# A streaming encoder layer: expert choices every 16 ticks, own buffers for the queries, and a mixer in three banks

## The reference, cut to what matters

```python
z = rmsnorm(h);  p = z @ W_in                       # W_in: 1024 x 3080, fp32
h = h + concat(rglru_group(p), mlstm_group(p)) @ W_out   # the mixer
h = h + peer(rmsnorm(h))
y = rmsnorm(h)

def peer_block(xb):                                 # xb: 128 tokens x 1024
    qh = (xb @ wq).reshape(128, 8, 2, 128)          # 8 heads, two halves
    s1, s2 = qh[:, :, 0] @ keys1.T, qh[:, :, 1] @ keys2.T    # 128 keys each
    v1, i1 = top_k(s1, 16);  v2, i2 = top_k(s2, 16)
    sc, ci = top_k((v1[..., :, None] + v2[..., None, :]).reshape(128, 8, 256), 16)
    e = take(i1, ci // 16) * 128 + take(i2, ci % 16)         # 16 experts a head
    act = gelu(einsum('td,thkd->thk', xb, u_tab[e])) * softmax(sc)
    return einsum('thk,thkd->td', act, v_tab[e])
```

## Time and profile before

| | |
|---|---|
| Median of three runs | 3309.66 us (3309.31 to 3315.91) |
| The profiled execution, its own time | 3304.53 us |
| Its span in the profile | 3302.3 us |
| TensorE, VectorE, ScalarE, GpSimd busy | 79%, 69%, 20%, 61% |
| Mean granted TensorE clock | 0.852 |
| Read from memory, mean rate | 1205.73 MB, 367 GB/s |

### The profile page before, as it was taken

One profiled execution on the slowest core, in us unless ns is written; L12 is line 12 of the kernel. 1 busy time (PEld: TensorE's weight loads), 2 busy tenths in 40 slices (PEclk: granted clock), 3 DMA queues, 4 the chain that ended last, 5 costly groups with the idle time before them and its releaser, 6 DMA issues.

```text
span 3302.3 us, 42154 instructions
## 1 busy us (share of the span) xinstructions
PE 2607.0 (79%) x11764; PEld 1183.6 (36%) x11764; DVE 2282.9 (69%) x6088; ACT 648.6 (20%) x2367; POOL 2004.0 (61%) x2131
## 2 busy tenths in 40 slices
PE   7687888778887788778887788778887788777666
PEld 2563453234422453234422453234422453233111
DVE  2454987678756887679756887578766887679453
ACT  2221222111211222111211122112211222111111
POOL 0132567665776567665766567665776567665775
PEclk9798999878997889878987899878997889888557
DMA  7354999999999999999999999999999999999998
GB/s 263 135 197 166 387 363 394 416 390 344 396 405 403 377 368 395 409 391 349 399 402 398 376 368 398 407 392 343 404 413 400 371 368 399 403 398 359 398 399 362
DMA packets 340171, 1213.81 MB, mean 368 GB/s; under 512 B 41072, under 2 KB 41200, under 8 KB 339904
## 3 DMA queue, kind: packets, MB, share of 16 engines
q0 software_dynamic: 304128, 1107.43, 85.8%
q1 hardware_dynamic: 35776, 103.32, 8.3%
HBM read 1205.73 MB, written 4.87 MB: 367 GB/s over the span
## 4 chain that ended last, share of the span: by engine, by line
PE 25%; DMA 25%; DVE 24%; issue 15%; POOL 6%; ACT 3%; POOLq 0%; DVEq 0%; ACTq 0%; SPq 0%
DMA ring<-peer_v,idxv 16%; PE bank L458 15%; PE acc L458 10%; DMA ring<-peer_u,idx 9%; DVE ring L1434 8%; POOL ring L434 6%; DVE kw L1211 2%; DVE eh L1222 1%; DVE kw L1221 1%; DVE topi L1213 1%; DVE kw L1219 1%; ACT xn L857 1%; DVE idxv L1269 1%; DVE tops L1212 1%; DVE topi L1214 1%
## 5 line engine op out<-in xcount | busy, mean ns | idle before, releaser
L458 PE MATMUL acc<-ring,wv 128*32 128x512 f32 x4224 | 1312.9, 709 | 540.4 <-DMA ring<-peer_v,idxv 417.7
L1434 DVE SCALAR_TENSOR_TENSOR ring<-ring,xcur 128x1024 f32<-128x1024 f32 x1056 | 1283.6, 1218 | 656.4 <-DMA ring<-peer_u,idx 630.6
L434 POOL DMA_INDIRECT ring<-peer_u,idx x1056 | 1006.6, 953 | 817.7 <-issue 416.3
L434 POOL DMA_INDIRECT ring<-peer_v,idxv x1024 | 964.0, 941 | 433.5 <-issue 277.1
L458 PEld LDWEIGHTS acc<-ring,wv 128*32 128x32 f32 x4224 | 171.3, 115 | 1203.2 <-issue 662.7
L458 PEld LDWEIGHTS bank<-xT,win 128*128 128x128 f32 (+1 forms) x2304 | 276.2, 190 | 108.5 <-issue 92.9
L458 PE MATMUL bank<-xT,win 128*128 128x128 f32 (+1 forms) x2304 | 307.1, 290 | 6.8 <-DVE kw L1232 4.3
L857 ACT ACTIVATE wv<-rep,coefv 128x32 f32<-128x32 f32 x1024 | 264.3, 312 | 109.4 <-PE acc L458 79.4
L458 PEld LDWEIGHTS bank<-xT,qk 128*128 128x128 f32 x1024 | 160.1, 246 | 64.5 <-issue 64.5
L458 PE MATMUL bank<-win,xT 128*128 128x512 f32 (+3 forms) x368 | 177.3, 614 | 1.9 <-ACT xT L857 1.9
L458 PE MATMUL bank<-xT,qk 128*128 128x128 f32 x1024 | 173.1, 338 | 0.0
(11 more groups left out here) (232 smaller groups left out, 2213.8 us busy)
## 6 DMA issues: line engine op xcount, KB each, us to landing
qk<-wq SPq DMA_DIRECT2D x64, 512.0 KB
t<-wq SPq DMA_DIRECT2D x64, 512.0 KB, 6.9
ring<-peer_u,idx POOLq DMA_INDIRECT x1056, 6.5
ring<-peer_v,idxv POOLq DMA_INDIRECT x1024, 6.6
win<-w_in SPq DMA_DIRECT2D x6, 2048.0 KB, 15.3
ring<-wq SPq DMA_DIRECT2D x16, 512.0 KB, 5.2
wout<-w_out SPq DMA_DIRECT2D x1, 4096.0 KB, 22.4
xn<-x_prompt SPq DMA_DIRECT2D x8, 512.0 KB, 6.9
```

The source lines that it names most:

```text
L434: pool.indirect_dma_start(out=ring[:, slot, :], out_offset=None, in_=(peer_u, peer_v)[which], in_offset=bass.IndirectOffsetOnAxis(ap=rows_ ...
L458: return nc.tensor.matmul(out, lhsT, rhs, start=start, stop=stop)
L1434: stt(row, row, 1.0, xcur[:, :], ALU.mult, ALU.mult, accum_out=dots[:, column(b, e):column(b, e) + 1]).then_inc(s_dot, 1)
```

## The change

- A head's choice comes every 16 ticks: head h's first query product at tick 16h - 22, the second 3 ticks later, the scores at 16h - 13, the five steps at 16h - 12 to 16h - 8, the spread at 16h - 7. Heads 0 and 1 begin in the block before.
- Queries get buffers of their own: `wqb` (one, not two), `x2T`, `q2`, `pick`, and the PSUM bank bQ, which also takes both spreads. The mixer has bA, bC and bD.
- The mixer's ticks move: norm at 24 (30), convolution 38 (44), recurrence 49 (55), values 62 (66), chunk 70 (74), output 87 (91), second norm 101 (105). The waits between mixer and spreads go; some inside the mixer come, as the value projection's on the recurrence (`s_m2`).
- The lookup of a choice is one one-hot product over 512 columns, where there were two over 256.
- The norms' weights are columns. The second norm's are applied by ScalarE as it moves the transposed x; TensorE transposes that back into `xcur` (`show_x`) and spreads the final norm's row into bA and bC each block (`final_row`). ScalarE scales by the second norm's rstd, not VectorE.
- x is loaded into `h`, after `take_up`, not into `xn` after the store of y.

```diff
 HEAD_TICKS = TOPK
 BLOCK_TICKS = PEER_HEADS * HEAD_TICKS
-QUERY_TICKS = 5
-T_QUERY = 1
-T_NORM, T_XT, T_XT_OUT = 30, 35, 36
+Q_FIRST, Q_SECOND, Q_SCORES, Q_CHOOSE, Q_GATE, Q_SPREAD = 0, 3, 9, 10, 13, 15
+Q_LEAD = 22
+EARLY_HEADS = (0, 1)
+T_NORM, T_XT, T_XT_OUT = 24, 29, 30
...
-T_XL, T_GATES, T_GL, T_Q, T_K, T_V, T_O = 37, 43, 45, 52, 59, 66, 73
-T_CONV = 44
-T_ROWS = 46
-T_GELU = 51
-T_LRU = 55
-T_CHUNK = 74
-T_OUT = 91
-T_NORM2 = 105
-T_QUERY0 = 110
+T_XL, T_GATES, T_GL, T_Q, T_K, T_V, T_O = 31, 37, 39, 46, 53, 62, 69
+T_CONV = 38
+T_ROWS = 40
+T_GELU = 45
+T_LRU = 49
+T_CHUNK = 70
+T_OUT = 87
+T_NORM2 = 101
...
-        ffn_bc = sb("ffn_bc", [P, D_MODEL])
-        final_bc = sb("final_bc", [P, D_MODEL])
+        ffn = sb("ffn", [P, CM])
+        fin = sb("fin", [P, CM])
+        wqb = sb("wqb", [P, CM, P])
+        x2T = sb("x2T", [P, CM, P])
+        q2 = sb("q2", [P, 2, P])
+        pick = sb("pick", [P, 2 * TOPK * TOPK])
...
-        wq_buf = [qk, t34]
-        q2 = G
...
-        bank = [ctx.enter_context(nc.psum_tensor(f"bank{b}", [P, 512], fp32)) for b in range(4)]
-        bA, bB, bC, bD = bank
+        bA, bC, bD, bQ = [ctx.enter_context(nc.psum_tensor(f"bank{b}", [P, 512], fp32)) for b in "ACDQ"]
+        num_banks, c_banks, out_banks, x2_banks = (bA, bD), (bC, bA), (bA, bC), (bD, bA)
...
+        def query_step(head, tick):
+
+            return tick + Q_LEAD - HEAD_TICKS * head
...
             def load_wq(b, tiles):
                 for ft in tiles:
-                    if ft < 2:
-                        sp.wait_ge(s_ym_ps, streams_before(b) + 1)
-                    else:
-                        sp.wait_ge(s_qp_ps, b * 16 + ft - 1)
+                    if ft or not is_count(b, 0):
+                        sp.wait_ge(s_qp_ps, b * 16 + ft)
                     held()
-                    sp.dma_start(wq_buf[ft % 2][:, :, :], wq[ft]).then_inc(s_wq[ft % 2], 16)
+                    sp.dma_start(wqb[:, :, :], wq[ft]).then_inc(s_wq, 16)
...
             def load_x(b, block):
 
-                sp.wait_ge(s_xcur, streams_before(b))
+                sp.wait_ge(s_acc0, b + 1)
                 held()
-                sp.wait_ge(s_y_out, 16 * b)
-                held()
-                sp.dma_start(xn[:, :], block).then_inc(s_x, 16)
+                sp.dma_start(h[:, :], block).then_inc(s_x, 16)
...
                     if part == 0:
                         pe.wait_ge(s_win[4], 16)
-                        pe.wait_ge(s_ri_exp, v + 1)
+                        pe.wait_ge(s_m2, v + 1)
...
+                for half, at in enumerate((Q_FIRST, Q_SECOND)):
+                    if step == at:
...
+                        for c in range(CM):
+                            last = mm(bQ[:, P * half:P * half + P], wqb[:, c, :], x2T[:, c, :], start=c == 0, stop=c == CM - 1)
+                        last.then_inc(s_qp_ps, 1)
+                if step == Q_SCORES:
...
+                if step == Q_SPREAD:
...
+                    spread_rows(ef[:, :], s_idx_ps)
...
+            def show_x(b):
+
+                pe.wait_ge(s_x2, streams_before(b) + 1)
+                if b is not None:
+                    pe.wait_ge(s_dot, experts_before(b))
+                for c in range(CM):
+                    last = nc.tensor.transpose(xcur[:, P * c:P * c + P], x2T[:, c, :], ident[:, :])
+                last.then_inc(s_xcur, 1)
+
+            def final_row(b):
+
+                n = n_experts(b)
+                if b is None:
+                    pe.wait_ge(s_rows_bc, 32)
+                for c in range(CM):
+                    last = mm(by4((bA, bC)[c // 4])[0:n, c % 4, :], spread(fin[:, c:c + 1], 1, n), ident[:, :])
+                last.then_inc(s_fin, 1)
...
+                if tick % TOPK == 1 and tick > TOPK:
+                    spread_coef(b, tick // TOPK - 1)
                 for head in range(1, PEER_HEADS):
-                    query(b, head, tick - T_QUERY - QUERY_TICKS * (head - 1))
...
+                    query(b, head, query_step(head, tick))
                 if more:
+                    for head in EARLY_HEADS:
+                        query(b + 1, head, query_step(head, tick - BLOCK_TICKS))
                     mixer(b + 3, b + 2, P, True, tick, b)
...
-                    rstd(n, 3, D_MODEL).then_inc(s_rstd2, 1)
+                    link(rstd(n, 3, D_MODEL))
+                    a(xn[0:n, :], h[0:n, :], ACT.Copy, scale=stat[0:n, 5:6]).then_inc(s_xn2, 1)
...
-            def take_over(b):
...
-                    last = a(xcur[:, :], xn[:, :], ACT.Copy)
-                last.then_inc(s_xcur, 1)
...
-                    pick(0, temps)
+                    oh = one_hots(temp)
+                    link(tt(oh, ci[:, 1:3, :].unsqueeze(3).to_broadcast(square),
+                            iota[:, :].unsqueeze(1).unsqueeze(1).to_broadcast(square), ALU.is_equal))
+                    link(tt(oh, oh, topi[:, :, :].unsqueeze(2).to_broadcast(square), ALU.mult))
                 if step == 4:
-                    pick(1, temps)
+                    link(dve.tensor_reduce(eh[:, :, :], one_hots(temp), AX.X, ALU.add))
...
-                stt(y, y, stat[0:n, 8:9], final_bc[0:n, :], ALU.mult, ALU.mult).then_inc(s_y, 1)
+                dve.wait_ge(s_fin, streams_before(b) + 1)
+                for half, bank in enumerate((bA, bC)):
+                    y = xn[0:n, 512 * half:512 * half + 512]
+                    last = stt(y, y, stat[0:n, 8:9], bank[0:n, :], ALU.mult, ALU.mult)
+                last.then_inc(s_y, 1)
```

356 lines of the change are left out of this document (152 added, 204 removed).

## The result

The changed kernel takes 3453.56 us (median of 5 runs, 3433.92 to 3471.85), the kernel before 3309.31 on the same chip: a ratio of 1.0439, 95% interval 1.0392 to 1.0486. It is slower by 4.4%; forecast was 3287 us and the range ended at 3358. The execution that was profiled is the longest of the five, 3471.85 us, so differences between the two profiles are some 20 us larger than those of the medians.

The account below looks back on a forecast made before the run. Memory and GpSimd's gather issue, both about 420 GB/s, were taken as the bound. Seven passes at -2.6 us, last block -13 and start +8 gave -23, so 3287 us against a 3309.7 median; range 3225 to 3358.

Parts of the forecast that it names:

- How much lateness is free: Ring of 8 row buffers: VectorE or TensorE may be 3 us late (2.2 to 4.5) at no cost, then all lost.
- Part 1: Choices every 16 ticks: late at most 2.8 us, heads 1 and 2 cost 0.3 each; -10.4 us a pass.
- Part 2: Choices meeting the mixer: head 3 at the convolution +4.9, head 4 at the recurrence +2.1, heads 5 to 7 +2.1 us.
- Removed 11.0: Dense choices, ticks 5 to 14 and 21 to 41: their whole loss of 11.0 us a pass would go.
- their count at half: Heads 5 to 7: 4.3 us lost, entered as +2.1 because their stretch already loses 5.5.
- Part 3: Queries on TensorE in the mixer, ticks 29 to 58: 81.3 us of work against 79.7 of traffic, +1.6 us.
- rival B: Thinner ring, only 2.2 us free: 3339 us; second half, TensorE over 95% busy in ticks 29 to 58: to 3365; chance 0.22.
- Part 4: Turn of the loop, ticks 15 to 20: -2.4 us without arrears, -1.0 if the final row keeps TensorE's clock up.
- Part 5: Small items: showing x by TensorE transposes +0.5 us; single query-weight buffer no price, 0 to 0.5 us a head.
- a sign that held: Start of the kernel: growing by over 15 us was listed as a sign of the forecast being wrong.
- C: TensorE's clock: thinned queries at half clock bind TensorE outside the mixer, some 9 us a pass, 3359 us; chance 0.05.
- A: Lumps are absorbed by the ring, 4.5 us free: -10 a pass, -16 in the last block, 3231 us; chance 0.17.

Follow-up runs that it names:

- packed: Changed kernel with each choice's five steps in 3 ticks instead of 5; 3591.72 us, ratio 1.0856.
- spaced_copy: spaced with VectorE's copy of the spread choice one tick behind TensorE's spreading product, second query product a tick later too; 3324.96 us, 1.0051.
- align: Changed kernel with each head's first query tile load held back until the scores of the head before are there; 3451.53 us, 1.0401.
- conv44: Changed kernel with the convolution at ticks 44 and 45 instead of 38 and 39; 3428.45 us, 1.0386.
- copy_conv44: spaced_copy with the convolution at ticks 44 and 45 instead of 38 and 39; 3308.79 us, 1.0003.
- o_later: two_at_start with the projection of o two ticks later (71 to 76 instead of 69 to 74); 3303.36 us, 0.9969.
- two_at_start: x_early with the very first block's second query tile loaded early into qk; 3301.89 us, 0.9959.
- turn: Changed kernel with the final norm weights' spread moved ahead to tick 10 and SP storing y before loading the next x; 3464.59 us, 1.0466.
- second5: Changed kernel with a head's second query product 5 ticks after its first instead of 3; 3456.72 us, 1.0438.
- x_early: copy_conv44 with the sample's h copied to the idle query-weight buffer, so the first block's x loads earlier; 3309.63 us, 1.0011.
- spaced: Changed kernel with each choice's five steps at about every second tick, copy and gate later to match; 3364.96 us, 1.0141.

## Why the prediction was wrong

**The step that failed: "How much lateness is free".** It put 8 slots x 1.245 = 9.96 us against 6.5 for a row to land and 1.3 to be used, and took 3 us as free, at every lump anew. The runs put 0.9 us lost for each microsecond late between 0.5 and 6.1 us at head 7, and an allowance of at most about 1 us. The 6.5 us are no fixed delay but grow with the queue: the first eight gathers of the changed kernel's sample, with nothing queued ahead of them, land after 4.8 us, all of its u gathers after 6.9, packed's after 6.6 and those of spaced_copy, which keeps memory busiest of the three, after 7.2 (medians). That the queue is what keeps memory busy while an engine is late, and that it isn't refilled, since GpSimd's 1.24 us a gather is no faster than memory, is shown by the rows of head 7; that it holds everywhere is my reading. So Part 1's "0.3 each" for heads that stand alone should have been nearly their whole lateness, and the same 3 us were missing in each lump of Part 2. The lateness itself was sized a little low: 2.8 forecast, 3.5 measured. As an estimate from the prediction's own terms, with nothing free: heads 1 and 2 cost 2.5 us more each, heads 3 and 4 cost 3 more each, and heads 5 to 7 cost 13.3 together, or 6.7 if still counted half, for 2.1. The sum is then +13 to +20 us a pass for -2.6. Measured were +17.9.

**Removed 11.0 (Part 1).** The three stretches lose 12.4 us now, where 11.0 were to go. Before, ticks 5 to 14 and 21 to 31 were dense and cheap, 1.7 and 1.5 us, and I read it so that memory had other work while VectorE was the bound: 34.4 us at 399 GB/s are 13.7 MB, 3.2 more than ten ticks of gathers, and 39.1 at 404 are 15.8, 4.3 more. Now it is 0.5 and 1.5 MB. No run puts a price on this cover; align shows that shifting half the loads doesn't bring it back.

**Part 2.** The convolution's meeting was priced at 4.9 us a pass; conv44 took 25 us out, 3.6 a pass, and copy_conv44 16, 2.3. Right in mechanism, and too dear by a quarter where a choice still takes five ticks in a row. A likely reason, not tested, is that what was thought free had been lost already. Ticks 42 to 60, forecast with 3.7 more (recurrence and TensorE), lose 6.4 more. Ticks 66 to 115, forecast with 2.1, lose 8.9 more: this holds heads 5, 6 and 7, and their count at half was the second largest error. The last block was forecast at -13 and loses 5.6 more.

**Part 3 and rival B's second half.** TensorE was busy 52.11 of 57.6 us in ticks 42 to 60, 90%, not over 95. It is fuller behind them: over seven passes it is busy 96% of ticks 64 to 76, which lose 4.6 us for 1.2 before. This part of rival B stays open for the changed kernel, since o_later, which left the time as it was, stands on two_at_start.

**Part 4.** The turn was forecast at -2.4 - 1.0 and measures -1.7. That the final row would keep the clock up was right for the clock: `take_up` took 2.13 us, not 3.73. It bought nothing: in turn it lay elsewhere, `take_up` took 3.98 us again, and gap and time were the same.

**Part 5.** "No price" for the single buffer held in the passes, though one tick less costs 2.2 us a head. The prediction named waits of the query products for their weights as a sign of being wrong; they came, 132 us of them, and second5 shows that they weren't the reason. In the start the same buffer cost x_early 7 us. The start was forecast 8 us longer and is 36 longer: this was a sign that held. 15 of them are head 1's query, held back until head 0's indices are copied.

**The rivals.** B was the right one, a ring with less to spare, but with 2.2 us free it ended at 3339 to 3365. It needed the case "nearly nothing is free". C is seen in the clock, 0.71 and 0.75 in ticks 5 to 20 and 0.64 in 21 to 31, for 0.90, 0.81 and 0.91 before. It is not seen in the time: these ticks lose 11.8 us where they lost 10.5. One pair of rows alone would mislead here. In spaced,

```profile
1857.00:1945.80 88.80, 57.59 (x230) 25.05 (x230) 53.38 (x141) 16.57 (x58) 52.25 (x56) 0.71 0.96 366
```

the clock is that of the changed kernel (0.70 in the same ticks), and in the pass shown of spaced_copy it is higher and the ticks are shorter:

```profile
1824.50:1908.50 84.00, 53.30 (x233) 22.39 (x234) 53.43 (x140) 16.68 (x58) 50.81 (x54) 0.84 0.95 370
```

Over seven passes ticks 5 to 31 have a clock of 0.71 in packed, 0.73 in the changed kernel, 0.76 in spaced_copy and 0.86 before, and lose 16.5, 12.4, 9.3 and 9.9 us. So with the clock still 0.10 lower than before they lose no more than before. Most of the 9.3 us are the turn (7.0 in ticks 15 to 20 of the pass shown), which leaves the clock some 2 us a pass at most. No run holds the clock fixed. The Trainium skill (TensorE: Matmul & The Clock Gate, section on HAM oscillation) says that waits between bursts of matmuls send the clock back down: the rows agree with that, as the queries were thinned out and the clock fell. That the time hardly followed fits with TensorE's idle time in those ticks, busy 53.30 of 84.00 us. A falls by the measure of head 7: with 4.5 us free, its 3.5 us of lateness would have cost nothing.

## What to carry to other kernels

Where transfers are the bound and the issuing engine is no faster than memory, price every microsecond by which a consumer falls behind at about its full length (0.9 of it here), and don't grant each lump a fresh allowance. The sum over a few ticks counts: spread an occasional job over as many ticks as its deadline leaves, one step and one breath, and put its waits for other engines a tick behind what they wait for. A long row in the waits view is a question, not an answer; one edit that removes it and nothing else tells its worth, here 120 us of waits for no gain at all. And ask what a slow stretch covers before it is thinned out: the dense choices of ticks 5 to 14 and 21 to 31 lost only 1.7 and 1.5 us, with 3.2 and 4.3 MB of other transfers beside the gathers.

## What was not expected of the hardware

- The hole in memory's traffic comes mostly behind the late engine: 408 GB/s in the choice and 350 after it. When packed it reaches into the choice, 356 GB/s, and is deeper behind it, 278.
- The query weights' load is harmless in the passes when due 3 ticks, 7.6 us, after it may start, and costs 2.2 us a head when due after 2 ticks, 5.1 us.
- The two norm weights as columns are 4 KB each, and SP spends 5.2 us on issuing either; they land after 14.6 and 10.6 us. Moved behind the next load they changed nothing in the time.
- At the turn the engines stand for 4.7 to 5.9 us between their last work and the first of the next pass (VectorE idle 5.00 us before the product of 1963.35, where it was 2.61 in the earlier trace rows). SP's transfers were moved away from there in two ways, with no effect on the time. The profile's DMA queues show three instruction fetches between 1957 and 1964 us, and as many at the shorter turn of the kernel before, between 1855 and 1862; no run tells whether they make the wait. The Trainium skill (Runtime: NRT & Kernel Launch, Instruction fetch mechanics) says that a taken branch to a place that isn't prefetched has to fetch it by DMA before it can go on; no run here unrolled the loop to try it.
